# Self-attention of a hybrid decoder trunk: row maximum, exponential and transposes one PSUM bank at a time

## The chip, the cores and the metric

The kernel runs on one core of one Trainium2 chip. The metric is the device time of one execution in microseconds (us); of several runs the median is taken. TensorE is called PE here (PEld is its weight load), VectorE is DVE, ScalarE is ACT, GpSimd is POOL, SyncE is SP. PSUM has eight banks of 512 f32 values in each of 128 partitions.

## The reference, cut to what matters

Two layers of a decoder with 1024 tokens. Each layer has a causal attention of 8 heads (head width 96 for q and k, 64 for v), a state-space group, a recurrent group, an output projection, a cross-attention and an MLP. The change touches only the causal attention:

```
for one block of 128 queries and one head:
    sc = q_i @ k^T * scale                 # 128 x 1024
    sc = where(kpos <= qpos, sc, -inf)     # so only (i+1)*128 columns count
    p  = softmax(sc) = exp(sc - max) / sum(exp(sc - max))
    y  = p @ v
```

## The kernel before, in words

All data stay in SBUF with the token or the channel on the partitions, and the weights stream in. The attention of a layer is written as 64 units, `unit(n)`: four pairs of heads, in each pair eight query blocks i = 0 to 7, in each block the two heads. Unit n works on w = (i+1)*128 key columns. For i below 4 (a short unit) the scores fill one PSUM bank or less, for i of 4 to 7 (a long unit, 32 in each layer) they reach into a second. Units alternate between banks 0, 1 and banks 2, 3. The number n mod 16 is the place of a unit in its pair of heads; places 8 to 15 are the long ones.

What a unit passes through, with its lines:

- PE `scores(n)`: one f32 product of up to 512 columns for each bank (L1191), and in the last bank a small bf16 product that adds the mask (L1194). It then counts up `s_ps`.
- DVE `row_max(n)`: waits for `s_ps`, one reduction over all w columns, across both banks (L2165). It writes the negated maximum `nmx`.
- ACT `probs(n)`: waits for `nmx`, one exponential over all w columns into `prob`, with the row sum into `esum` (L1702). It counts up `s_exp`.
- PE `probs_T(n)`: waits for `s_exp`, transposes `prob` in chunks of up to four 128x128 blocks (L1207). The chunks alternate between banks 4 and 5; chunk m also waits until the copy of chunk m-2 is done (`pt_sb`).
- ACT `keep_probs_T(n)`: copies each chunk to SBUF (L1737).
- PE `outputs(g)`: after every four units, probabilities times values (L1221).

The order on each engine is written out by hand, and each engine works its own list in order. PE does scores(n+1), then sometimes outputs, then a side task, then probs_T(n). ACT does probs(n+1), a side task, then keep_probs_T(n): so the copies of unit n stand behind the exponential of unit n+1. DVE does row_max(n+1), then side tasks. The side tasks (`side_tasks`) are the q and k projections of the next heads and the state-space chunks: EL and EA (exponentials on ACT, L1718, L1722), CB and TR (DVE), Y (PE L1163, DVE L2197 and L2203), RB (the reciprocal sums: PE L1178, ACT L1726, after which DVE scales y, L2175).

POOL runs its own list beside them, mostly products and sums of two SBUF tensors: `rope_add` (L788, 32 partitions x 1024), `ssd_inputs` (L762), `decay_products` (L751, L754), `gate_z` (L795), `y_square` (L802, L805, L807), and in the last pair of heads `split_early` (L812, L815) and `split_lru` (L823, L825), which prepare operands of the output projection.

`recip_sums` (L2169) takes the reciprocal of the eight sums of half a pair of heads. `nmx`, `mx`, `rsum` and `rinv` are small SBUF tables, [128, 2, 4]; `esum` is [128, 2, 8].

Of the kernel before, what the change touches and what calls it, by code (L numbers as in the profile page):

```python
# [21 lines left out]
ALU = mybir.AluOpType  # L22
ACT = mybir.ActivationFunctionType
AX = mybir.AxisListType


P = 128
DEPTH = 2
T = 1024
HT = 512  # L30
# [35 lines left out]
def step(n):  # L66

    return n // STEPS, n % STEPS
# [62 lines left out]
def unit(n):  # L131

    return n // (2 * NBLK), (n % (2 * NBLK)) // 2, n % 2


def chunks_before(n):

    return sum(1 if unit(m)[1] < 4 else 2 for m in range(n))
# [61 lines left out]
def x_tile(n):  # L200
# [17 lines left out]
             "mix_gt": 4, "mix_rstd": 3, "mg_hi": 1, "xk_done": 8, "mv_done": 2, "mv_lo": 4, "xpt_lo": 8, "xs_exp": 8, "xpt_sb": 8, "xo_hi": 16,  # L218
             "sum_y": 4, "sum_hi": 16, "hm_sq": 64, "p1_kept": 15, "t_free0": 16, "t_free1": 16, "h_lo": 24,
             "sq_used": 24, "sum_ready": 6, "softplus_v": 3, "k_rot": 1, "conv_done": 6, "lru_xr": 2, "lru_v": 4,  # L220
             "prep": 1, "first_qk_dve": 4, "s_max": 64, "side_dve": 36, "m_ce": 8, "m_sw": 8, "m_xd": 8, "r_inv": 8,
             "m_st": 8, "y_done": 8, "mix_sum": 2, "mix_lo": 6, "mix_n": 6, "mg_v": 1, "mg_lo": 1, "xq_done": 8,
             "xs_max": 8, "xp_n": 8, "xo_lo": 16, "sum_v": 16, "hm_t": 64, "x_add": 17, "c_add": 105, "mem_sq": 2,
             "mem_sum": 1, "mem_col": 1, "mem_rstd": 1, "hm_st": 768, "a_hi": 161, "a_lo": 161, "a_sum": 60,
# [28 lines left out]
def trunk(nc, xT, memT, posb, ropec, small, final_g, wt, wv, wh, lruw, outT):  # L253
# [7 lines left out]
    def sem(name):  # L261
        return ctx.enter_context(nc.semaphore(name))

    with ctx:
# [27 lines left out]
        prob = at("prob", B + 24 * K, [P, 2, T])  # L292
# [75 lines left out]
        mx = at("mx", o + 340, [P, 2, 4])  # L368
        nmx = at("nmx", o + 372, [P, 2, 4])
        rsum = at("rsum", o + 404, [P, 2, 4])  # L370
# [4 lines left out]
        esum = at("esum", o + 760, [P, 2, NBLK])  # L375
# [4 lines left out]
        ps = ctx.enter_context(nc.psum_tensor("ps", [P, 8, HT], F32))  # L380

        def banks(b, n=2):
            return ps[:, b:b + n, :].rearrange("p b t -> p (b t)")
# [46 lines left out]
        dt_ps, prep = sem("dt_ps"), sem("prep")  # L430
# [2 lines left out]
        q_rope, q_half, k_rope, k_rope_1, k_rot = (sem(n) for n in ("q_rope", "q_half", "k_rope", "k_rope_1", "k_rot"))  # L433
        side_ps, side_a, side_v = sem("side_ps"), sem("side_act"), sem("side_dve")
        s_ps, s_max, s_exp, pt_ps, pt_sb, o_ps = (sem(n) for n in ("s_ps", "s_max", "s_exp", "pt_ps", "pt_sb", "o_ps"))
        r_inv, y_done, y_sq, y_acc = sem("r_inv"), sem("y_done"), sem("y_sq"), sem("y_acc")
        m_aU, m_cz, m_ce, m_sw, m_xd, m_st, m_z = (
            sem(n) for n in ("m_aU", "m_cz", "m_ce", "m_sw", "m_xd", "m_st", "m_z"))
# [39 lines left out]
        def cols_of(half):  # L478
            return slice(half * HT, (half + 1) * HT)

        def stat(t, n):

            i = (n // 2) % t.shape[2]
            return t[:, n % 2, i:i + 1]

        def here(counted, n, of_layer=None):

            return n + PER_LAYER[counted.name] * (layer if of_layer is None else of_layer)

        with nc.Block() as block:  # L490
# [44 lines left out]
            for layer in range(DEPTH):  # L535
# [421 lines left out]
                def _(pe):  # L957
# [116 lines left out]
                    for b in range(NBLK):  # L1074
                        last = pe.transpose(ps[:, 6, b * 32:(b + 1) * 32], ss[0:32, b * P:(b + 1) * P], ident[0:32, 0:32])
# [107 lines left out]
                    def scores(n):  # L1183

                        c, i, hh = unit(n)
                        q, k = qT[c % 2][hh], kT[c % 2][hh]
                        for j in range(0, i + 1, 4):
                            w = min(4, i + 1 - j) * P
                            dst = ps[:, 2 * (n % 2) + j // 4, 0:w]
                            edge = j + 4 > i  # L1190
                            last = pe.matmul(dst, q[0:DQ, i * P:(i + 1) * P], k[0:DQ, j * P:j * P + w],  # L1191
                                             start=True, stop=not edge)
                            if edge:
                                last = pe.matmul(ps[:, 2 * (n % 2) + j // 4, w - P:w], ident_h[:, :], future[:, :],  # L1194
                                                 start=False, stop=True)
                        last.then_inc(s_ps, 1)

                    def probs_T(n):

                        i = unit(n)[1]  # L1200
                        pe.wait_ge(s_exp, here(s_exp, n + 1))
                        for part, j0 in enumerate(range(0, i + 1, 4)):
                            m = chunks_before(n) + part
                            if m >= 2:
                                pe.wait_ge(pt_sb, here(pt_sb, m - 1))
                            for j in range(j0, min(j0 + 4, i + 1)):
                                last = pe.transpose(ps[:, 4 + m % 2, (j - j0) * P:(j - j0 + 1) * P],  # L1207
                                                    prob[:, n % 2, j * P:(j + 1) * P], ident[:, :])
                            last.then_inc(pt_ps, 1)
# [58 lines left out]
                    for j, (src, bank) in enumerate(((sq, 4), (ss, 6), (acc, 0))):  # L1268
# [8 lines left out]
                        for half in range(2):  # L1277
                            last = pe.matmul(ps[:, bank + half, :], ones[:, 0:1].to_broadcast([P, P]), src[:, cols_of(half)],
                                             start=True, stop=True)
# [21 lines left out]
                    for at_k in range(2, DC):  # L1301
# [5 lines left out]
                        for s in range(2):  # L1307
                            last = mix_products(s, at_k, 0, 1)
# [138 lines left out]
                    for s in range(2):  # L1447
# [7 lines left out]
                        w = wsp[:, s, :, :].rearrange("p a (k m) -> p a k m", m=P)  # L1455
                        for half in range(2):
                            for k in range(DC):
                                for part, a in ((0, 0), (0, 1), (1, 0)):
                                    last = pe.matmul(ps[:, 2 + half, :], w[:, part, k, :], hB[:, a, k, cols_of(half)],
                                                     start=(k == 0 and part == 0 and a == 0), stop=(k == DC - 1 and part == 1))  # L1460
# [90 lines left out]
                    for n in range(RING_FILLS):  # L1551
# [9 lines left out]
                        for q in (0, 1, 3, 2):  # L1561
                            if n == 0 and q == 2:
                                pe.wait_ge(ht_sum, here(ht_sum, 4 * NFP - 1))
                            last = operand_products(n, q)
                        last.then_inc(u_done, 1)
                    operands_ready(FILLS - 1)
                    for q in range(4):
                        if last_layer and q == 2:
                            fin_means(0)
                        for n in range(RING_FILLS, FILLS):  # L1570
                            last = operand_products(n, q)
# [6 lines left out]
                def _(act):  # L1578
# [117 lines left out]
                    def probs(n):  # L1696

                        w = (unit(n)[1] + 1) * P
                        act.wait_ge(s_max, here(s_max, n + 1))
                        if n >= 2:  # L1700
                            act.wait_ge(pt_ps, here(pt_ps, chunks_before(n - 1)))
                        act.activation(prob[:, n % 2, 0:w], banks(2 * (n % 2))[:, 0:w], ACT.Exp,  # L1702
                                       bias=stat(nmx, n), accum_out=stat(esum, n)).then_inc(s_exp, 1)

                    def side_act(kind, i):
# [276 lines left out]
                def _(dve):  # L1982
# [109 lines left out]
                    for k in range(2):  # L2092
                        last = dve.scalar_tensor_tensor(cq_s[:, k, :], cq_s[:, k, :], g("q_g", k), banks(4), ALU.mult, ALU.mult)
# [49 lines left out]
                    for ch in range(2):  # L2143
                        last = dve.scalar_tensor_tensor(gt_s[:, ch, :], gt_s[:, ch, :], g("lru_g", ch), banks(4), ALU.mult, ALU.mult)
# [15 lines left out]
                        dve.tensor_tensor(turned[NOPE:DQ, cols], ps[DQ:P, bank, :], cs[half][DQ:P, :], ALU.mult).then_inc(done, 1)  # L2160

                    def row_max(n):
                        dve.wait_ge(s_ps, here(s_ps, n + 1))
                        w = (unit(n)[1] + 1) * P
                        dve.tensor_reduce(stat(nmx, n), banks(2 * (n % 2))[:, 0:w], AX.X, ALU.max, negate=True).then_inc(s_max, 1)  # L2165

                    def recip_sums(hf):
                        dve.wait_ge(s_exp, here(s_exp, 8 * hf + 8))
                        dve.reciprocal(rinv[:, :, :], esum[:, :, 4 * (hf % 2):4 * (hf % 2) + 4]).then_inc(r_inv, 1)  # L2169

                    def keep_y(hf):
# [132 lines left out]
                    for c in range(DC):  # L2304
                        if c in (4, DC - 1):
                            n = c // 4 - (c == 4)
# [178 lines left out]
                    for n in range(2, FILLS):  # L2485
                        operand_low(n)
                        p, i = step(n - SLOTS + 1 - STEPS)
# [133 lines left out]
```

## Time and profile before

| | us |
|---|---|
| median of 3 runs | 2822.7 |
| lowest, highest | 2820.27, 2824.53 |
| the profiled execution | 2822.41 |
| its span | 2820.7 |
| PE busy in it | 2755.8 (98%) |
| DVE busy | 1477.2 (52%) |
| ACT busy | 1153.2 (41%) |
| POOL busy | 1551.8 (55%) |

The granted clock of TensorE is 0.996 of full speed over the span. "Busy" is the union of an engine's recorded instructions. Times of single rows are microseconds from the start of the span. A matmul's recorded end is modelled: in a stream without a pause the next f32 matmul of 128 columns is recorded as starting a little before the end of the one before.

### The profile page before, as it was taken

How to read it: one execution, taken by the hardware profiler on the slowest of the kernel's cores; microseconds unless marked ns; L12 is line 12 of the kernel's file. 1: busy time of each engine (PE TensorE's matmuls, PEld its weight loads, DVE VectorE, ACT ScalarE, POOL GpSimd, SP SyncE). 2: the span in 40 equal slices, each digit the busy share in tenths (PEclk: the TensorE clock that was granted, in tenths of full speed). 3: DMA queues.
4: the chain of work that ended last, by engine and by line, in shares of the span. 5: the costliest groups of instructions: out<-in, count | busy, mean ns of one | idle time of the engine just before them, and what ended most of it. 6: DMA issues, size and time to landing. Idle time of an engine off the chain costs nothing.

```text
span 2820.7 us, 33795 instructions
## 1 busy us (share of the span) xinstructions
PE 2755.8 (98%) x12974; PEld 2165.7 (77%) x12974; DVE 1477.2 (52%) x1575; ACT 1153.2 (41%) x1802; POOL 1551.8 (55%) x887
## 2 busy tenths in 40 slices
PE   8999999999999999999999999999999999999998
PEld 6766668888878887888887666688888788878886
DVE  8584456116474555445665744561265755455445
ACT  3455552224153434333324655432242434343334
POOL 4333443450357776697833344434413777767977
PEclk9999999999999999999999999999999999999999
DMA  3100011230124447676311000112201343476763
GB/s 139 50 10 6 16 38 42 78 105 8 52 95 163 145 142 242 199 243 208 110 62 42 15 1 16 39 51 90 90 16 45 127 153 139 161 248 196 237 203 119
DMA packets 175402, 292.17 MB, mean 104 GB/s; under 512 B 16656, under 2 KB 84240, under 8 KB 174608
## 3 DMA queue, kind: packets, MB, share of 16 engines
q1 hardware_dynamic: 175248, 290.08, 30.9%
q8 instruction: 101, 1.65, 0.2%
q14 instruction: 53, 0.43, 0.1%
HBM read 226.85 MB, written 63.18 MB: 103 GB/s over the span
## 4 chain that ended last, share of the span: by engine, by line
PE 85%; DVE 8%; ACT 3%; POOL 1%; issue 1%; DMA 1%; SPq 0%; DVEq 0%; ACTq 0%; POOLq 0%
PE ps L1528 21%; PE ps L1468 18%; PE ps L969 18%; PE ps L1337 6%; PE ps L1191 4%; PE ps L1221 2%; PE ps L1393 2%; PE ps L1207 2%; PE ps L1352 2%; PE ps L1368 2%; PE ps L1085 2%; DVE hT L2376 1%; DVE xbc L2056 1%; PE ps L1420 1%; PE ps L1287 1%
## 5 line engine op out<-in xcount | busy, mean ns | idle before, releaser
L1528 PE MATMUL ps<-b_op,a_op 128*128 128x512 f32 x2688 | 614.6, 391 | 11.6 <-POOL a_op L910 8.3
L1528 PEld LDWEIGHTS ps<-b_op,a_op 128*128 128x128 f32 x2688 | 506.5, 189 | 119.2 <-POOL a_op L910 9.2
L969 PE MATMUL ps<-hA,wsp 128*128 128x512 f32 x1920 | 442.3, 391 | 0.8 <-POOL wsp L724 0.7
L721 POOL TENSOR_TENSOR wsp<-raw,ones 128x1024 fp32r<-128x1024 f32 x63 | 124.4, 1975 | 555.6 <-PE ps L969 446.2
L969 PEld LDWEIGHTS ps<-hA,wsp 128*128 128x128 f32 x1920 | 360.3, 188 | 80.7 <-issue 5.3
L2420 DVE TENSOR_TENSOR b_op<-raw_b,b_op 128x1024 fp32r<-128x1024 f32 x112 | 226.6, 2024 | 294.8 <-ACT b_op L1915 294.8
L1468 PE MATMUL ps<-hT,ring 128*128 128x512 f32 x1440 | 339.2, 394 | 8.1 <-POOL ring L878 8.1
L1468 PEld LDWEIGHTS ps<-hT,ring 128*128 128x128 f32 x1440 | 270.0, 189 | 75.0 <-POOL ring L878 19.6
L1915 ACT ACTIVATE b_op<-raw_b 128x1024 fp32r<-128x1024 f32 x112 | 118.8, 1061 | 335.1 <-PE ps L1528 305.1
L1468 PE MATMUL ps<-hB,ring 128*128 128x512 f32 x1080 | 250.6, 389 | 1.1 <-POOL ring L878 1.1
L1468 PEld LDWEIGHTS ps<-hB,ring 128*128 128x128 f32 x1080 | 202.6, 188 | 44.0 <-POOL ring L878 2.0
L910 POOL TENSOR_TENSOR a_op<-kept_a,a_op 128x1024 fp32r<-128x1024 f32 x64 | 203.1, 3180 | 33.5 <-ACT a_op L1920 32.7
L878 POOL TENSOR_TENSOR ring<-raw,ring 128x512 fp32r<-128x512 f32 x112 | 156.7, 1399 | 93.0 <-ACT ring L1888 88.0
L732 POOL TENSOR_TENSOR wsp<-raw,wsp 128x1024 fp32r<-128x1024 f32 x45 | 107.7, 2394 | 136.5 <-ACT wsp L1809 133.8
L1337 PE MATMUL ps<-hA,wsp 128*128 128x512 f32 x768 | 178.1, 391 | 0.1
L724 POOL TENSOR_TENSOR wsp<-raw,wsp 128x1024 fp32r<-128x1024 f32 x63 | 167.0, 2650 | 4.9
L878 POOL TENSOR_TENSOR ring<-blk_e,ring 128x512 fp32r<-128x512 f32 x98 | 126.6, 1292 | 76.2 <-ACT ring L1888 71.8
L1337 PEld LDWEIGHTS ps<-hA,wsp 128*128 128x128 f32 x768 | 143.6, 188 | 31.5 <-issue 1.9
L2165 DVE TENSOR_REDUCE nmx<-ps 128x1 f32<-128x256 f32 (+7 forms) x128 | 96.7, 757 | 133.1 <-PE ps L1194 131.3
L910 POOL TENSOR_TENSOR a_op<-raw_a,a_op 128x1024 fp32r<-128x1024 f32 x48 | 122.7, 2557 | 75.0 <-ACT a_op L1920 75.0
L969 PE MATMUL ps<-hB,wsp 128*128 128x512 f32 x672 | 155.2, 391 | 2.1 <-DVE x L2274 2.1
L2448 DVE TENSOR_TENSOR mu<-mu,ps 128x512 f32<-128x512 f32 x90 | 62.0, 689 | 169.4 <-PE ps L1468 167.4
(335 smaller groups left out, 4426.9 us busy)
## 6 DMA issues: line engine op xcount, KB each, us to landing
raw_b<-hidden_operands SPq DMA_DIRECT2D x112, 512.0 KB, 4.9
raw<-in_weight_tiles SPq DMA_DIRECT2D x108, 512.0 KB, 3.2
raw_a<-in_weight_tiles SPq DMA_DIRECT2D x192, 256.0 KB, 3.3
hidden_operands<-hm_t SPq DMA_DIRECT2D x128, 256.0 KB, 3.6
hidden_operands<-hm_s SPq DMA_DIRECT2D x96, 256.0 KB, 2.0
raw<-in_weight_tiles SPq DMA_DIRECT2D x64, 256.0 KB, 3.2
blk_e<-in_weight_tiles SPq DMA_DIRECT2D x56, 256.0 KB, 3.3
kept_a<-in_weight_tiles SPq DMA_DIRECT2D x32, 256.0 KB, 6.0
```

The costliest lines, as they stand in the source:

```text
L721: pool.tensor_tensor(wsp[:, s, 0, :], raw[:, s, :], ones[:, 0:1].to_broadcast([P, TILE]), ALU.mult).then_inc(w_ready[s], 1)
L724: pool.tensor_tensor(wsp[:, s, 1, :], raw[:, s, :], wsp[:, s, 0, :].bitcast(F32), ALU.subtract).then_inc(w_ready[s], 1)
L732: pool.tensor_tensor(wsp[:, s, 1, :], raw[:, s, :], wsp[:, s, 0, :].bitcast(F32), ALU.subtract).then_inc(w_ready[s], 1)
L878: pool.tensor_tensor(ring[:, FILL_SLOT[i], 1, :], pair_blk(g, src), ring[:, FILL_SLOT[i], 0, :].bitcast(F32), ALU.subtract).then_inc(a_lo, 1)
L910: pool.tensor_tensor(op[:, 1, :, :], source_a(n)[:, :, :], op[:, 0, :, :].bitcast(F32), ALU.subtract)\
L969: last = pe.matmul(ps[:, 2 * buf + half, 0:n], w[:, k, col:col + P], rhs(part, k, half * n, n), start=(at_k == 0 and w is w_hi and part == 0),
L1191: last = pe.matmul(dst, q[0:DQ, i * P:(i + 1) * P], k[0:DQ, j * P:j * P + w], start=True, stop=not edge)
L1337: last = pe.matmul(ps[:, 2 * (g % 2) + half, :], w[:, part, k, :], hA[:, a, k, half * HT:(half + 1) * HT], start=(k == 0 and part == 0 and ...
L1468: last = pe.matmul(ps[:, M_BANK[p], :], w[:, part, k, :], rhs(a, k), start=(k == 0 and part == 0 and a == 0), stop=(k == 3 and part == 1))
L1528: last = pe.matmul(ps[:, 4 * (1 - p % 2) + q, :], w[:, part, q // 2, r, (q % 2) * P:(q % 2 + 1) * P], h[:, a, r, :], start=(s == 0 and r = ...
L1915: act.activation(b_op[op_slot(n)][:, 0, :, :], raw_b[n % SLOTS][:, :, :], ACT.Copy).then_inc(b_hi, 1)
L2420: dve.tensor_tensor(op[:, 1, :, :], raw_b[n % SLOTS][:, :, :], op[:, 0, :, :].bitcast(F32), ALU.subtract)\
```

## The change

For long units the work goes bank by bank. PE counts up a new semaphore `s_ps_a` after the product of the first bank. DVE reduces the first bank as soon as that is there, into the table `mx`; then the second bank into `nmx`; then it waits for its own two results and joins them with a minimum (both are negated) of two 128x1 SBUF operands. ACT takes the exponential of the first bank and then of the second, as two instructions with a sum each: the first sum goes to `rsum`, the second to `esum`. PE may begin the transposes of the first four blocks after the first exponential (`s_exp_a`) and those of the rest after the second. Before the reciprocal of a half whose units are long, DVE adds the two tables of sums. Short units do what they did.

```
 def scores(n):
+    else:                                   # not the last bank
+        last.then_inc(s_ps_a, 1)
 def probs_T(n):
-    pe.wait_ge(s_exp, here(s_exp, n + 1))
     for part, j0 in enumerate(range(0, i + 1, 4)):
+        if part == 0 and i >= 4:
+            pe.wait_ge(s_exp_a, here(s_exp_a, long_before(n) + 1))
+        else:
+            pe.wait_ge(s_exp, here(s_exp, n + 1))
 def probs(n):
-    act.activation(prob[:, n % 2, 0:w], banks(2 * (n % 2))[:, 0:w], ACT.Exp,
+    if unit(n)[1] < 4:
+        act.activation(prob[:, n % 2, 0:w], ps[:, 2 * (n % 2), 0:w], ACT.Exp,
+                       bias=stat(nmx, n), accum_out=stat(esum, n)).then_inc(s_exp, 1)
+        return
+    act.activation(prob[:, n % 2, 0:HT], ps[:, 2 * (n % 2), :], ACT.Exp,
+                   bias=stat(nmx, n), accum_out=stat(rsum, n)).then_inc(s_exp_a, 1)
+    act.activation(prob[:, n % 2, HT:w], ps[:, 2 * (n % 2) + 1, 0:w - HT], ACT.Exp,
                    bias=stat(nmx, n), accum_out=stat(esum, n)).then_inc(s_exp, 1)
 def row_max(n):
+    w = (unit(n)[1] + 1) * P
+    if unit(n)[1] < 4:
+        dve.wait_ge(s_ps, here(s_ps, n + 1))
+        dve.tensor_reduce(stat(nmx, n), ps[:, 2 * (n % 2), 0:w], AX.X, ALU.max, negate=True).then_inc(s_max, 1)
+        return
+    dve.wait_ge(s_ps_a, here(s_ps_a, long_before(n) + 1))
+    dve.tensor_reduce(stat(mx, n), ps[:, 2 * (n % 2), :], AX.X, ALU.max, negate=True).then_inc(s_mx, 1)
     dve.wait_ge(s_ps, here(s_ps, n + 1))
-    w = (unit(n)[1] + 1) * P
-    dve.tensor_reduce(stat(nmx, n), banks(2 * (n % 2))[:, 0:w], AX.X, ALU.max, negate=True).then_inc(s_max, 1)
+    dve.tensor_reduce(stat(nmx, n), ps[:, 2 * (n % 2) + 1, 0:w - HT], AX.X, ALU.max, negate=True).then_inc(s_mx, 1)
+    dve.wait_ge(s_mx, here(s_mx, 2 * long_before(n) + 2))
+    dve.tensor_tensor(stat(nmx, n), stat(nmx, n), stat(mx, n), ALU.min).then_inc(s_max, 1)
 def recip_sums(hf):
     dve.wait_ge(s_exp, here(s_exp, 8 * hf + 8))
+    if hf % 2:
+        dve.tensor_tensor(esum[:, :, 4:8], esum[:, :, 4:8], rsum[:, :, :], ALU.add).then_inc(s_sum2, 1)
+        dve.wait_ge(s_sum2, here(s_sum2, hf // 2 + 1))
```

## Rows read from the trace of the kernel before

**Rows 1.** Stretches of the pairs of heads, layer 0: length, busy (count) by engine.

```profile
197.00:249.00 52.00, 50.69 (x312) 31.56 (x312) 23.71 (x46) 32.69 (x76) 23.24 (x24) 1.00 0.03 7
249.00:301.00 52.00, 51.00 (x328) 31.80 (x326) 22.22 (x44) 30.31 (x70) 21.80 (x21) 1.00 0.00 1
...
353.00:402.00 49.00, 43.70 (x322) 28.92 (x320) 23.62 (x40) 25.14 (x58) 28.93 (x22) 1.00 0.00 1
```

**Rows 2.** Timeline, unit 30: start, length, engine, line [idle before <-releaser].

```profile
290.79 1.22 DVE L2165 TENSOR_REDUCE nmx<-ps 128x1 f32<-128x1024 f32 x1 [4.50 <-PE ps L1194]
292.05 1.11 ACT L1702 ACTIVATE prob<-ps,nmx 128x1024 f32<-128x1024 f32 x1 [2.24 <-DVE nmx L2165]
293.16 0.97 ACT L1737 ACTIVATE probT<-ps 128x512 f32<-128x512 f32 x2
293.89 0.30 PE L1207 MATMUL ps<-ident,prob 128*128 128x128 f32 x1 [0.26 <-ACT probT L1737]
```

**Rows 3.** Groups by shape, DVE, whole span: count | busy, mean ns | idle before.

```profile
L2165 DVE TENSOR_REDUCE nmx<-ps 128x1 f32<-128x1024 f32 x16 | 19.6, 1225 | 35.8 <-PE ps L1194 35.8
L2165 DVE TENSOR_REDUCE nmx<-ps 128x1 f32<-128x512 f32 x16 | 11.1, 692 | 25.1 <-PE ps L1194 25.1
L2165 DVE TENSOR_REDUCE nmx<-ps 128x1 f32<-128x256 f32 x16 | 6.7, 421 | 9.5 <-PE ps L1194 9.2
L2165 DVE TENSOR_REDUCE nmx<-ps 128x1 f32<-128x128 f32 x16 | 4.5, 291 | 3.7 <-PE ps L1194 2.5 <-DVE xbc L2203 1.2
```

**Rows 4.** Groups by shape, ACT line L1702, whole span.

```profile
L1702 ACT ACTIVATE prob<-ps,nmx 128x1024 f32<-128x1024 f32 x16 | 17.8, 1115 | 23.9 <-DVE nmx L2165 23.9
...
L1702 ACT ACTIVATE prob<-ps,nmx 128x512 f32<-128x512 f32 x16 | 11.0, 688 | 9.0 <-DVE nmx L2165 8.8
```

**Rows 5.** Timeline, 59 to 64 us, small DVE instructions beside POOL.

```profile
59.22 1.89 POOL L721 TENSOR_TENSOR wsp<-raw,ones 128x1024 fp32r<-128x1024 f32 x1 [6.03 <-PE ps L969]
59.31 1.82 DVE L2001 TENSOR_TENSOR lr<-lr,c 128x2 f32<-128x2 f32 x1
61.16 0.16 DVE L2002 SCALAR_TENSOR_TENSOR c<-spt,lr 128x2 f32<-128x2 f32 x1
61.19 2.39 POOL L724 TENSOR_TENSOR wsp<-raw,wsp 128x1024 fp32r<-128x1024 f32 x1
61.36 2.25 DVE L2072 TENSOR_SCALAR c<-c 128x2 f32<-128x2 f32 x1
```

**Rows 6.** Timeline, units 26 and 27.

```profile
278.03 0.59 ACT L1726 ACTIVATE rbs<-ps 128x512 f32<-128x512 f32 x1
279.33 0.95 DVE L2165 TENSOR_REDUCE nmx<-ps 128x1 f32<-128x768 f32 x1
280.31 0.90 ACT L1702 ACTIVATE prob<-ps,nmx 128x768 f32<-128x768 f32 x1 [1.04 <-DVE nmx L2165]
281.68 0.87 ACT L1737 ACTIVATE probT<-ps 128x512 f32<-128x512 f32 x2
282.42 0.84 PE L1207 MATMUL ps<-ident,prob 128*128 128x128 f32 x6
```

**Rows 7.** Timeline, unit 12.

```profile
229.43 2.37 POOL L788 TENSOR_TENSOR qT<-qT,q_tmp 32x1024 f32<-32x1024 f32 x1
229.62 1.09 DVE L2165 TENSOR_REDUCE nmx<-ps 128x1 f32<-128x896 f32 x1 [1.69 <-PE ps L1194]
230.74 1.01 ACT L1702 ACTIVATE prob<-ps,nmx 128x896 f32<-128x896 f32 x1 [0.54 <-DVE nmx L2165]
```

**Rows 8.** Timeline, unit 56.

```profile
368.62 0.82 DVE L2165 TENSOR_REDUCE nmx<-ps 128x1 f32<-128x640 f32 x1
369.32 1.89 POOL L812 TENSOR_TENSOR w_early<-raw_early,ones 128x1024 fp32r<-128x1024 f32 x1
369.48 0.79 ACT L1702 ACTIVATE prob<-ps,nmx 128x640 f32<-128x640 f32 x1 [1.41 <-DVE nmx L2165]
371.39 1.74 PE L1221 MATMUL ps<-probT,v_tok 128*64 128x256 f32 x16 [0.48 <-ACT probT L1737]
```

More of the change, by code:

```diff
@@ L133, in unit, with long_before @@
     return n // (2 * NBLK), (n % (2 * NBLK)) // 2, n % 2
+def long_before(n):
+    return sum(1 for m in range(n) if unit(m)[1] >= 4)
 def chunks_before(n):
@@ L220 @@
              "sq_used": 24, "sum_ready": 6, "softplus_v": 3, "k_rot": 1, "conv_done": 6, "lru_xr": 2, "lru_v": 4,
-             "prep": 1, "first_qk_dve": 4, "s_max": 64, "side_dve": 36, "m_ce": 8, "m_sw": 8, "m_xd": 8, "r_inv": 8,
+             "prep": 1, "first_qk_dve": 4, "s_max": 64, "s_ps_a": 32, "s_mx": 64, "s_exp_a": 32, "s_sum2": 4, "side_dve": 36, "m_ce": 8, "m_sw": 8, "m_xd": 8, "r_inv": 8,
              "m_st": 8, "y_done": 8, "mix_sum": 2, "mix_lo": 6, "mix_n": 6, "mg_v": 1, "mg_lo": 1, "xq_done": 8,
@@ L435, in trunk @@
         s_ps, s_max, s_exp, pt_ps, pt_sb, o_ps = (sem(n) for n in ("s_ps", "s_max", "s_exp", "pt_ps", "pt_sb", "o_ps"))
+        s_ps_a, s_mx, s_exp_a, s_sum2 = (sem(n) for n in ("s_ps_a", "s_mx", "s_exp_a", "s_sum2"))
         r_inv, y_done, y_sq, y_acc = sem("r_inv"), sem("y_done"), sem("y_sq"), sem("y_acc")
```

## The prediction

> **What bounds the kernel now.** I read the page first: PE is busy 98% of the span, and most of the chain that ended last is PE, so a change is worth what it does to PE's pauses. The change touches only the attention, so I cut that into its four pairs of heads. [rows 1] gives, after the length of each stretch, the busy time of PE, PEld, DVE, ACT and POOL. PE lacks 1.31, 1.00 and 5.30 us in the first, second and last pair, and the third repeats the second (1.00): 8.6 us in layer 0. Layer 1 has the same pattern at the same places, so about 17 us of pauses lie in reach, 0.6% of the time. Everywhere else in the attention PE works without a pause, and what DVE and ACT do there is hidden as long as they are not later than PE.
>
> Then I went along PE's pauses in the timeline. In each of the first three pairs three of them stand at the end, places 14 and 15 (0.2 to 0.5 us each). The rest are in the last pair. [rows 2] shows the kind, unit 30, place 14: the reduction runs 290.79 to 292.01, the exponential follows at 292.05 for 1.11 us, then ACT goes straight into the two copies of the transposes of unit 29 (293.16), and PE begins the transposes of unit 30 at 293.89. The first copy takes half of the 0.97 us and ends at about 293.65; PE comes 0.2 us after that. So PE waits here for the copy that frees the bank, and this copy stands on ACT behind the whole exponential. The reader is to see that an early release of the first half of the exponential does not reach PE in such a place.
>
> **The change part by part.**
>
> *Reductions.* One reduction of 1024 columns costs 1.225 us, one of 512 0.692, of 256 0.421, of 128 0.291 [rows 3]; for 384 I take 0.56, midway between 256 and 512. If the first bank is reduced while PE still works on the second, only the second reduction lies after the scores, plus the join. The join is a DVE instruction of 128x1 on two SBUF operands. The nearest row is 0.16 us for 128x2 (the instruction at 61.16) [rows 5]; with 0.03 for its wait 0.20 us. So the exponential starts 1.225 - 0.692 - 0.20 = 0.33 us earlier for i = 7, and by the same slope for i = 6. For i = 4 the second product is over long before the first reduction is, and nothing is won; for i = 5 about 0.18.
>
> *Exponentials.* 1024 columns cost 1.115 us, two of 512 cost 2 x 0.688 = 1.376 [rows 4]: 0.26 us more, which is the part of an instruction that does not grow with its columns, so I take the same for every long unit. ACT starts its next instruction at the end of these lengths, so I take them whole. It comes to 64 x 0.26 = 17 us on ACT, which is 60% busy here [rows 1]; only the places count where PE stands behind ACT.
>
> *Net on the chain of [rows 2].* The start is 0.33 earlier, the end 0.26 later on top: the copy, and PE behind it, come 0.07 us earlier. This is nearly nothing, 0.07 in each of the first three pairs.
>
> *Place 11 (units 11, 27, 43).* [rows 6], unit 27: the reduction begins at 279.33 not because of the scores but because DVE has just scaled y, which waited for ACT's instruction at 278.03, which stood behind the exponential of unit 26. That one ends 0.22 later after the change (0.26 longer, 0.04 earlier), so the reduction begins at 279.55. Both halves then lie in series: 0.692 + 0.03 + 0.421 + 0.03 + 0.16 = 1.33 against 0.95; the exponential starts at 280.93 instead of 280.31, ends 0.26 later on top, and with the side exponential behind it the copies come at 282.56 instead of 281.68, 0.88 later. PE's transposes at 282.42 follow the first copy without any slack (PE has no pause there now, but the copy ends only 0.11 us before the first weight load), so PE is delayed 0.84. In sum + 0.8 in each of the first three pairs.
>
> *The join beside POOL.* [rows 5] shows DVE instructions of 128x2 with SBUF operands. 0.16 us is what they take undisturbed. The one at 59.31 takes 1.82 and ends at 61.13, POOL's two-operand instruction having run 59.22 to 61.11; the one at 61.36 takes 2.25 under POOL's next, which ends at 63.58. One that asks between the two gets through (61.16). So an instruction with two SBUF operands that asks after POOL has begun waits until about 0.14 before POOL's recorded end, whatever its size. The reductions from PSUM run beside POOL at their usual length [rows 7, 8]. The join is of the first kind, and it is new on the path; the units before the change had nothing of the sort there.
>
> I laid the 64 joins of the timeline against POOL. Most fall free. *Unit 12* [rows 7]: second reduction over at 229.62 + 0.56 = 230.18, the join asks at 230.21. POOL's L788 runs 229.43 to 231.80 (0.22 later after the change, since it hangs on the scaled y). The join ends at about 232.04, the exponential starts at 232.08 instead of 230.74, and ends 0.26 later on top: + 1.6. Side exponential, copies and PE follow, since ACT has no pause there. This takes the 0.84 of unit 11 into itself: 1.5 for the first pair. In the second and third pair L788 comes after the join of place 12, so they stay at 0.8.
>
> *Unit 56* [rows 8]: DVE comes free at about 368.5, reduces 0.69 and 0.29, the join asks at 369.54, POOL's L812 has begun at 369.32 and ends at 371.21. The join ends at 371.24; the exponential starts at 371.28 instead of 369.48 and ends at + 2.06. On ACT the side exponential and the copy of unit 55 follow directly, and PE's outputs at 371.39 already wait for that copy: + 2.05 us. Here L812 hangs on the same DVE instruction that frees DVE for the reductions, so the two keep their distance.
>
> *The rest of the last pair*: unit 59 repeats place 11 (+ 0.84), but PE's pause of 0.5 us before the outputs behind it takes most of it. For units 61, 62 and 63 it depends on tenths of a microsecond whether the join falls beside one of POOL's long instructions; free it is + 0.1, held + 1.9 at the end. I take 0.95. Last pair: 3.0.
>
> *The other edits.* The added PE waits stand in PE's queue ahead of instructions that already have one; beside the present double wait of probs_T PE runs on without a pause, so nothing; if not, 64 times a few hundredths. The eight added sums of tables stand before the reciprocals, may be held up to 0.7 us by L795, and are followed by RB 5 us later: nothing. What waits behind a held join on DVE are side tasks with more than 1 us to spare.
>
> **The sum.** One layer: 1.5 + 0.8 + 0.8 + 3.0 = 6.1; both 12.2. After the attention PE's chain goes on without a reserve that could take it back. On the profiled execution: 2822.4 + 12.2 = 2834.6; that execution lies 0.3 below the median, so 2835.
>
> The Trainium skill (GPSIMD Engine Reference, Specifications) says that POOL's SBUF interfaces are shared with VectorE, with contention for DVE instructions that have two SBUF inputs. It gives no price. Read as sharing cycles, it would have the join merely lengthened by its own 0.16 us, and the sum would be that of the first rival; the trace says it is held to the end of POOL's instruction.
>
> **The rivals.** (a) *The join is not held*, being only one column, or the joins fall between POOL's instructions. For: one at 61.16 got through. Against: 128x2 is nearly as small and was held. Only place 11 is left, 0.8 x 3 - 0.07, and about 0.1 in the last pair: 2.5 a layer, 2828. (b) *All joins of the last pair are held*: 1.5 + 0.8 + 0.8 + 2.05 + 1.9 = 7.1 a layer, 14 us, and a further one elsewhere 1 or 2 more: 2837 to 2840. (c) *Faster*: the first exponential releases the transposes of places 14 and 15, because the exponential and not the copy is PE's gate. Then PE comes 0.33 + 1.115 - 0.688 = 0.76 earlier in each of three pairs, about 1.5 in the last, 3.8 a layer: 2815, if place 11 costs nothing. For: the profile names the exponential as what the weight loads waited for. Against: [rows 2], PE starts half a microsecond after the exponential's end and 0.2 after the first copy's. It decides if the transposes of unit 30 start before the first copy.
>
> **How the numbers follow.** Forecast 0.55, (a) 0.2, (b) 0.14, (c) 0.11. The bounds of the last pair (2.1 to 4.0) and of unit 12 (0.8 to 1.5) alone give 9 to 14 us; (a) reaches down to 5, place 11 with some slack to 3. Range 2826 to 2841. What the measurement tells from no change is 0.2%, 5.6 us, here 2828.3; (a) is split by it. Faster 0.1, the same 0.15, slower 0.75.
>
> **What would show it.** Right: joins of 0.16 us mostly, of 1 to 2 us at units 12 and 56; the exponential of unit 27 at + 0.6; PE's pause before the outputs of unit 56 grown by 2 us; PE's first transposes of place 14 unmoved against its scores. Wrong: all joins short (then (a)); the transposes of unit 30 before the first copy (then (c)); a reduction of 512 columns slowed while PE writes the next bank.

## The result and the profile after

| | before | after |
|---|---|---|
| median, us | 2822.70 (5 runs) | 2840.40 (6 runs) |
| lowest, highest | 2820.27, 2824.63 | 2837.03, 2841.93 |
| the profiled execution | 2822.41 | 2838.73 |
| its span | 2820.7 | 2837.0 |
| PE busy | 2755.8 | 2760.1 |
| DVE busy | 1477.2 | 1517.8 |
| ACT busy | 1153.2 | 1167.9 |

The change makes the kernel slower: ratio 1.0062, with a 95% interval of 1.0051 to 1.0072. One run of the kernel before (3464.89 us) and one of experiment 8 (3463.72 us) fell into a slow state of the chip and are left out of the medians. I forecast + 12.2 us; the profiled execution shows + 16.3 and the medians + 17.7. The direction and most of the mechanism held; a term of about 5 us was missing.

Where the time went is read first by pairs, as in [rows 1]. The cuts are moved by the delay that had built up. The columns are again the length, and the busy time of PE, PEld, DVE, ACT and POOL; the number ahead of the DMA share is the granted clock.

```profile
197.00:251.00 54.00, 51.48 (x318) 31.89 (x317) 28.00 (x63) 34.18 (x92) 23.04 (x24) 1.00 0.03 7
251.00:305.00 54.00, 52.51 (x329) 32.61 (x330) 25.80 (x61) 32.14 (x86) 21.84 (x21) 1.00 0.00 1
305.00:358.00 53.00, 51.50 (x336) 32.58 (x336) 26.05 (x62) 32.91 (x88) 23.14 (x22) 1.00 0.06 21
358.00:412.00 54.00, 45.28 (x304) 29.44 (x302) 32.30 (x57) 26.32 (x72) 28.92 (x22) 0.91 0.00 1
```

PE now lacks 2.52, 1.49, 1.50 and 8.72 us, against 1.31, 1.00, 1.00 and 5.30: + 1.21, + 0.49, + 0.50 and + 3.42. The reader is to see the last line's clock too, 0.91 where [rows 1] has 1.00. The whole attention of each layer, cut at the same instructions in both kernels, splits the loss into pauses and slower work. First the changed kernel, layer 0 and layer 1, same columns:

```profile
196.77:411.75 214.98, 200.74 (x1276) 126.39 (x1276) 112.38 (x242) 125.78 (x338) 97.18 (x89) 0.98 0.02 7
1599.55:1821.25 221.70, 207.47 (x1305) 129.84 (x1304) 116.21 (x246) 131.50 (x345) 101.63 (x91) 0.98 0.04 12
```

and the kernel before:

```profile
197.00:402.00 205.00, 196.39 (x1276) 124.14 (x1276) 91.78 (x174) 118.44 (x274) 97.08 (x89) 1.00 0.03 8
...
1590.00:1805.00 215.00, 206.41 (x1305) 129.17 (x1304) 95.58 (x178) 124.13 (x281) 101.67 (x91) 0.99 0.04 12
```

The number of products is the same (1276 and 1305). What PE lacks went from 8.61 to 14.24 in layer 0 and from 8.59 to 14.23 in layer 1: pauses + 11.3 us together. The same products took 4.35 and 1.06 us longer: + 5.4. That is 16.7; 0.4 of it comes back outside the attention.

**The groups** (form xcount | busy, mean ns of one | idle before) answer to [rows 3, 4]:

```profile
L2186 DVE TENSOR_REDUCE mx<-ps 128x1 f32<-128x512 f32 x64 | 44.1, 689 | 47.5 <-PE ps L1197 45.6
L2190 DVE TENSOR_TENSOR nmx<-nmx,mx 128x1 f32<-128x1 f32 x64 | 34.3, 536 | 2.2
L1717 ACT ACTIVATE prob<-ps,nmx 128x512 f32<-128x512 f32 x64 | 44.1, 689 | 81.4 <-DVE nmx L2190 81.1
L1719 ACT ACTIVATE prob<-ps,nmx 128x512 f32<-128x512 f32 x16 | 10.9, 679 | 0.0
```

The reduction of 512 columns costs 0.689 with PE writing the bank beside it, against 0.692 in [rows 3], so PE's writes do not slow it. The join costs 0.536 on average, where a free one has 0.16: the mean hides two kinds. Of the 64 joins 24 begin while a POOL instruction runs that has more than 0.2 us left; all 24 last until that instruction's recorded end and 0.01 to 0.02 us more. The other 40 take 0.16 to 0.18. Which of the held ones cost time has to be looked for one by one in the timeline (start, length; in brackets the idle time and its releaser). Unit 12, the answer to [rows 7]:

```profile
229.38 0.56 DVE L2188 TENSOR_REDUCE nmx<-ps 128x1 f32<-128x384 f32 x1
229.40 2.35 POOL L794 TENSOR_TENSOR qT<-qT,q_tmp 32x1024 f32<-32x1024 f32 x1
229.97 1.80 DVE L2190 TENSOR_TENSOR nmx<-nmx,mx 128x1 f32<-128x1 f32 x1
231.81 0.69 ACT L1717 ACTIVATE prob<-ps,nmx 128x512 f32<-128x512 f32 x1 [1.12 <-DVE nmx L2190]
```

A join of one column, begun at 229.97, ends at 231.77, with POOL's instruction (231.75). Unit 56, against [rows 8], is the same thing and the dearest:

```profile
371.41 1.89 POOL L818 TENSOR_TENSOR w_early<-raw_early,ones 128x1024 fp32r<-128x1024 f32 x1
371.64 1.68 DVE L2190 TENSOR_TENSOR nmx<-nmx,mx 128x1 f32<-128x1 f32 x1
373.35 0.69 ACT L1717 ACTIVATE prob<-ps,nmx 128x512 f32<-128x512 f32 x1 [3.19 <-DVE nmx L2190]
...
375.51 2.79 PE L1232 MATMUL ps<-probT,v_tok 128*64 128x256 f32 x12 [2.49 <-ACT probT L1754]
```

Unit 30, against [rows 2]: a free join, two exponentials in a row, then the copies, then PE.

```profile
293.27 0.16 DVE L2190 TENSOR_TENSOR nmx<-nmx,mx 128x1 f32<-128x1 f32 x1
293.47 0.69 ACT L1717 ACTIVATE prob<-ps,nmx 128x512 f32<-128x512 f32 x1 [1.91 <-DVE nmx L2190]
294.15 0.68 ACT L1719 ACTIVATE prob<-ps,nmx 128x512 f32<-128x512 f32 x1
294.81 0.98 ACT L1754 ACTIVATE probT<-ps 128x512 f32<-128x512 f32 x2
295.55 0.63 PE L1218 MATMUL ps<-ident,prob 128*128 128x128 f32 x4 [0.16 <-ACT probT L1754]
```

PE's transposes come 0.74 after the copy has begun and 1.39 after the first exponential's end. The early release is not used: in both layers the transposes of places 14 and 15 start 0.74 us after the first of these copies, as in the kernel before.

The delay of PE's first transposes against the kernel before, taken unit by unit from start times, gives the ladder. Layer 0: + 0.49 at unit 11, + 1.31 at 12, + 1.21 from 14; + 1.93 at 27, + 1.66 from 30; + 2.39 at 43, + 2.12 from 46; + 5.74 at 56, + 6.20 at 60, + 7.42 at 63; PE is + 9.75 when the attention is over (it transposes the reciprocals at 411.44, before at 401.69). In layer 1 the first pair costs 1.44 and the second and third 0.45 each again, unit 56 costs 2.02 and not 3.62, and the end is at + 16.22 (1814.34 against 1798.12).

**The missing part** shows where the clock is cut finely. Same columns, the changed kernel:

```profile
370.00:375.60 5.60, 3.05 (x17) 1.76 (x17) 5.39 (x8) 2.27 (x7) 4.80 (x3) 1.00 0.02 3
375.60:379.00 3.40, 3.40 (x17) 1.98 (x18) 0.25 (x2) 1.13 (x4) 0.13 (x1) 0.50 0.00 0
402.90:409.70 6.80, 4.99 (x24) 3.29 (x26) 1.56 (x4) 2.66 (x6) 0.00 (x0) 0.50 0.00 0
1805.80:1812.60 6.80, 4.97 (x22) 3.28 (x24) 1.58 (x4) 2.68 (x6) 0.00 (x0) 0.50 0.00 0
```

0.50 of full speed is the lower level, 1.2 GHz. Until 375.51 PE had stood for 2.49 us; until 401.60 it had stood for 1.93, ahead of the second fall, and inside that stretch it stands 1.36 more. The kernel before has one such stretch in the two attentions, 3.4 us from 1793.4, behind pauses of 0.58, 1.48 and 0.74 us; behind nearly the same three in layer 0 (0.59, 1.48 and 0.74) it has none. PE's work inside runs at half speed: 3.40 + 4.99 + 4.97 - 3.40 = 10.0 us of it more than before, half of that is 5.0 us, and 5.4 is what the same products took longer. The other runs of the changed kernel have a mean clock of 0.992 to 0.995, the profiled one 0.995, so some of them probably hold more such stretches; they have no trace.

### The profile page after: what moved, and what is told of

It is laid out like the page before. It is cut to its first block, busy times and chain, and to the rows that moved or that the text cites. A ratio compares the mean times of both kernels' runs of the same rounds, so it can differ in the third digit from the quotient of the medians.

```text
span 2837.0 us, 34123 instructions
## 1 busy us (share of the span) xinstructions
PE 2760.1 (97%) x12974; PEld 2167.0 (76%) x12974; DVE 1517.8 (54%) x1711; ACT 1167.9 (41%) x1930; POOL 1551.7 (55%) x887
## 4 chain that ended last, share of the span: by engine, by line
PE 83%; DVE 9%; ACT 4%; POOL 1%; issue 1%; DMA 1%; SPq 0%; DVEq 0%; ACTq 0%; POOLq 0%
PE ps L1539 21%; PE ps L1479 18%; PE ps L975 17%; PE ps L1348 6%; PE ps L1197 3%; PE ps L1232 2%; PE ps L1404 2%; PE ps L1363 2%; PE ps L1379 2%; PE ps L1091 2%; PE ps L1218 1%; DVE hT L2404 1%; DVE xbc L2073 1%; PE ps L1431 1%; PE ps L1298 1%
## 5 line engine op out<-in xcount | busy, mean ns | idle before, releaser
L975 PEld LDWEIGHTS ps<-hB,wsp 128*128 128x128 f32 x672 | 126.0, 188 | 29.9 <-issue 3.8
```

Of the source, the lines that this page charges most:

```text
L975: last = pe.matmul(ps[:, 2 * buf + half, 0:n], w[:, k, col:col + P], rhs(part, k, half * n, n), start=(at_k == 0 and w is w_hi and part == 0),
```

## The experiments

The comparisons have their own runs of the kernel before, with medians of 2822.36 to 2822.44.

**1. The join by another instruction.** Both halves' maxima lie side by side, and one reduction over two columns with a single SBUF input joins them.

```
-         mx = at("mx", o + 340, [P, 2, 4])
-         nmx = at("nmx", o + 372, [P, 2, 4])
+         both = at("both", o + 340, [P, 2, 2, 4])
+         mx, nmx = both[:, 0, :, :], both[:, 1, :, :]
...
- dve.tensor_tensor(stat(nmx, n), stat(nmx, n), stat(mx, n), ALU.min)
+ dve.tensor_reduce(stat(nmx, n), both[:, :, n % 2, (n // 2) % 4], AX.X, ALU.min)
```

> The changed kernel with its join written as a reduction over two columns of one SBUF table (one SBUF input) instead of a minimum of two SBUF operands. Nothing else differs. Theory (the join is held by POOL because it has two SBUF inputs): a reciprocal with one SBUF input ran beside POOL at its usual 0.2 us, so all 128 joins take about 0.2 us; unit 12 and unit 56 lose nothing, PE's long pauses of the last pair go, and with them the half-speed stretches of TensorE. What is left is place 11 and the longer exponentials: 0.45 in each of the first three pairs, about 0.3 in the last, so 2 to 4 us above the kernel before, some 2826. Rival (the two exponentials on ACT are the cost): as slow as the changed kernel, 2840, joins short or not. Rival (any small SBUF instruction on DVE is held): joins still 1 to 2 us at units 12 and 56, 2840.

Measured: 2825.14, ratio 1.0011 (1.0002 to 1.0020). The long units are 32 a layer, so there are 64 joins and not the 128 that the expectation says. Their group in this kernel:

```profile
L2190 DVE TENSOR_REDUCE both<-both 128x1 f32<-128x2 f32 x64 | 9.9, 155 | 2.2
```

Not one is held: at unit 12 it begins at 229.41 under a POOL instruction that runs from 228.83 for 2.36 us, and takes 0.16. Here too 24 of the 64 begin while a POOL instruction has more than 0.2 us left, and each of them takes 0.15 to 0.16. So about 15 of the 17.7 us go with the form of one tiny instruction. What is left is + 0.4 a pair, from place 11, and 0.49 at unit 56. The expectation missed in one point: half-speed stretches do not all go. In the profiled execution 3.4 us of layer 0's attention and 6.8 of layer 1's run at half speed, against 3.4 in all before.

It is shown that this form of the join is not held, and that neither its size nor its wait nor the moment was the cause. The edit changes two things at once, the operation and the number of SBUF inputs, and the trace of the kernel before separates them:

```profile
199.97 1.04 POOL L762 TENSOR_TENSOR aU_lo<-tri_le,att_l 128x512 fp32r<-128x512 f32 x1
200.46 0.69 DVE L2156 TENSOR_TENSOR q_tmp<-ps,cs 64x512 f32<-64x512 f32 x1 [1.34 <-PE ps L1085]
...
371.29 2.36 POOL L815 TENSOR_TENSOR w_early<-raw_early,w_early 128x1024 fp32r<-128x1024 f32 x1
371.69 0.19 DVE L2169 RECIPROCAL rinv<-esum 128x8 f32<-128x8 f32 x1
```

A TENSOR_TENSOR with one input in PSUM runs at its usual 0.69 beside POOL, so it is not the operation as such. Of the TENSOR_TENSORs with both inputs in SBUF that begin there while a POOL instruction has more than 0.2 us left, 119 of them, none ends before POOL's. But one SBUF input is not enough to be free. The reciprocal above is, and the reduction. The TENSOR_SCALAR at 61.36 in [rows 5] has one SBUF input as well and was held for 2.25 us, and so was a copy from SBUF to SBUF (L2213, which still runs 0.55 us after POOL's end).

**2. Exponentials split, one reduction.** No join.

```
- dve.wait_ge(s_ps_a, ...); dve.tensor_reduce(stat(mx, n), ...)
- dve.wait_ge(s_ps, ...);   dve.tensor_reduce(stat(nmx, n), ...)
- dve.wait_ge(s_mx, ...);   dve.tensor_tensor(...)
+ dve.wait_ge(s_ps, here(s_ps, n + 1))
+ dve.tensor_reduce(stat(nmx, n), banks(2 * (n % 2))[:, 0:w], AX.X, ALU.max, negate=True)
```

> The exponentials and transposes bank by bank as in the changed kernel, with the two sums, but the row maximum as one reduction as before: no join. Theory: only the 0.26 us more on ACT per long unit counts. At places 14 and 15 PE stands behind ACT, + 0.26 there; at place 11 two exponentials and the scaled y in a chain, + 0.5. So + 0.5 to 0.8 a pair of heads, 4 to 6 us in all, 2828. Rival (exponentials are the whole cost): 2840. Rival (c) of the prediction (the early release helps PE): below 2822.

Measured: 2827.47, ratio 1.0018 (1.0008 to 1.0028), + 5.1 us. Unit 30 here:

```profile
293.36 0.68 ACT L1717 ACTIVATE prob<-ps,nmx 128x512 f32<-128x512 f32 x1
294.02 0.98 ACT L1752 ACTIVATE probT<-ps 128x512 f32<-128x512 f32 x2
294.76 1.06 PE L1216 MATMUL ps<-ident,prob 128*128 128x128 f32 x8 [0.51 <-ACT probT L1752]
```

PE starts 0.74 after the first copy has begun, as in every kernel here that leaves ACT's order alone. The split exponential brings nothing and costs 0.26 where ACT is what PE waits for: + 0.55 a pair.

**3. Reductions split, one exponential, the join with two inputs.**

```
- act.activation(prob[:, n % 2, 0:HT], ...).then_inc(s_exp_a, 1)
- act.activation(prob[:, n % 2, HT:w], ...)
+ act.activation(prob[:, n % 2, 0:w], banks(2 * (n % 2))[:, 0:w], ACT.Exp, ...)
...                                       # PE waits for s_exp alone
```

> The row maximum bank by bank with the two-operand join as in the changed kernel, but one exponential and one wait of PE as before. Theory: the holds stay. Unit 12 about + 1.0 us, unit 56 + 1.8, units 61 to 63 one or two holds more, and TensorE falls to half speed after the longer pauses; places 14 and 15 gain 0.3 a pair. Each layer + 4 to 6 us, 8 to 12 in all, 2833. Rival (exponentials are the cost): at or below the kernel before, 2820 to 2823.

Measured: 2836.04, ratio 1.0043 (1.0029 to 1.0057). The joins have a mean of 535 ns again; up to unit 12 1.0 us is lost, and at unit 56 3.2 to 3.4, its join taking 1.68 and a half-speed stretch following in both layers. In its profiled execution four stretches at half speed lie in the two attentions, 20.5 us in sum.

**4. The same with the join of experiment 1.**

```
- dve.tensor_tensor(stat(nmx, n), stat(nmx, n), stat(mx, n), ALU.min)
+ dve.tensor_reduce(stat(nmx, n), both[:, :, n % 2, (n // 2) % 4], AX.X, ALU.min)
```

> The row maximum bank by bank with the join as a reduction of one SBUF input, one exponential as before. Theory: neither holds nor longer exponentials. Places 14 and 15 start 0.3 us earlier, place 11 (DVE busy before it) is up to 0.4 later, the last pair gains about 0.3: in sum within 3 us of the kernel before, likelier below it, 2821. Rival (any small SBUF instruction is held): as the third kernel, 2833. Rival (the reading of one bank by DVE while PE writes the next slows one of them): the scores or the first reductions take longer than before and the time is above 2828.

Measured: 2819.86, ratio 0.9994 (0.9985 to 1.0003). Per pair + 0.20 at place 11, then - 0.15 and - 0.34 at places 12 and 14; no stretch at half speed in either attention. Against experiment 3 this is one instruction for another, and 16 us. The early reduction was the good part of the change: in PE's start times it gains about 0.3 in a pair. In the time of the whole kernel that is not clear of the noise, as the interval holds 1.

**5. Only unit 56's join with two inputs.** Experiment 1 with

```
+ if n == 56:
+     dve.tensor_tensor(...)      # the join of the change
+ else:
+     dve.tensor_reduce(...)      # the join of experiment 1
```

> The first experiment (all joins as reductions, both exponentials) with the two-operand join put back in unit 56 alone, once in each layer. Theory: that join asks 0.2 us after POOL's L812 has begun and is held 1.5 us; PE's outputs of unit 56 come 2.0 us later than in the first experiment in both layers. In layer 0 of the changed kernel TensorE fell to half speed for 3.41 us right behind this pause and 3.6 us were lost instead of 2.0: if the pause is what brings that, it shows again here, in sum 4 us above the first experiment plus up to 1.7 us for each half-speed stretch of 3.41 us that is added: 2829 to 2833. Rival (the clock falls through something else, later joins or chance): 2.0 us in each layer and no stretch at 375 us, 2829.

Measured: 2833.33, ratio 1.0036 (1.0022 to 1.0049): 8.2 us above experiment 1 for two held joins, one in each layer, which are 1.5 us each longer than a free one (1.68 against 0.16). The five runs fall into two sorts: 2829.43 and 2830.04 at a mean clock of 0.995 and 0.996, and 2833.33, 2833.99 and 2834.04 at 0.993 and 0.994. The profiled one is the lowest. In it

```profile
370.71 1.68 DVE L2191 TENSOR_TENSOR both<-both 128x1 f32<-128x1 f32 x1
...
374.59 1.63 PE L1232 MATMUL ps<-probT,v_tok 128*64 128x256 f32 x14 [2.50 <-ACT probT L1754]
```

PE stands 2.50 us before the outputs that follow unit 56's scores, and no half-speed stretch follows in layer 0 (+ 1.99 from unit 48 to 56); in layer 1 the same pause is followed by one (+ 3.52). The pause does not decide it alone. Only the lowest has a trace, so where the clock fell in the others is not seen. The two tables lie side by side here as in experiment 1, so their place in SBUF was not what cured the join. The price of a held join is its delay in some executions, and more where TensorE's clock falls behind it.

**6. POOL starts after the join.** The change as it is, and POOL's first instruction of that place waits for the join of unit 56.

```
+ pool.wait_ge(s_max, here(s_max, 57))
  split_early(0, w_early)
```

> The changed kernel with one wait added on POOL: the first instruction of the early weight split (L812 of the kernel before) waits until the join of unit 56 is done, once in each layer. DVE, ACT and PE are as in the changed kernel, two-operand joins included. Theory: the join of unit 56 takes 0.16 us instead of 1.68, PE's outputs of unit 56 come 2 us earlier in each layer, and where the half-speed stretch behind it goes, 1.7 us more; the join of unit 57 may now be held by the next instruction of POOL, which has 1.7 us of slack before PE. In sum 3 to 7 us below the changed kernel, 2833 to 2837. Rival (the joins are slow by themselves, not through POOL): unchanged, 2840.

Measured: 2834.58, ratio 1.0040 (1.0026 to 1.0053), 5.8 us below the changed kernel.

```profile
371.68 0.16 DVE L2191 TENSOR_TENSOR nmx<-nmx,mx 128x1 f32<-128x1 f32 x1
371.92 1.89 POOL L818 TENSOR_TENSOR w_early<-raw_early,ones 128x1024 fp32r<-128x1024 f32 x1 [0.43 <-DVE nmx L2191]
...
374.03 1.73 PE L1233 MATMUL ps<-probT,v_tok 128*64 128x256 f32 x16 [0.97 <-ACT probT L1755]
```

The join takes 0.16 and unit 56 costs 0.47 and 0.49 in the two layers. The later holds stay: the joins of units 60 to 63 take 0.70, 2.24, 1.59 and 1.19 beside POOL's later instructions, as in the changed kernel (0.71, 2.25, 1.60, 1.19), and 10.2 us in each layer run at half speed around the attention's end, where the changed kernel has 6.8. A two-input join is cured by order only one place at a time.

**7. Early reduction only where it gains.** Experiment 4 for query blocks 6 and 7; the others as in the kernel before, one reduction and one wait.

```
- return sum(1 for m in range(n) if unit(m)[1] >= 4)
+ return sum(1 for m in range(n) if unit(m)[1] >= 6)
...
- if unit(n)[1] < 4:
+ if unit(n)[1] < 6:
```

> The fourth experiment (row maximum bank by bank, join as a reduction, one exponential) but only for query blocks 6 and 7, where the scores of the second bank take longest; blocks 4 and 5 have one reduction as before. Theory: place 11 no longer pays its 0.2 us and places 14 and 15 keep their 0.34 in each pair: about 0.2 x 3 x 2, 1 us better than the fourth experiment, 2818 to 2820. Rival (place 11's loss was made good at place 12 anyway): equal to the fourth.

Measured: 2819.53, ratio 0.9989 (0.9980 to 0.9998). The profiled execution, 2814.89, is the lowest of eleven, with no stretch at half speed in either attention.

```profile
290.18 0.15 DVE L2182 TENSOR_REDUCE both<-both 128x1 f32<-128x2 f32 x1
290.37 1.11 ACT L1711 ACTIVATE prob<-ps,both 128x1024 f32<-128x1024 f32 x1 [1.90 <-DVE both L2182]
292.21 1.06 PE L1216 MATMUL ps<-ident,prob 128*128 128x128 f32 x8
```

Place 11 costs nothing now and places 12 and 14 keep their gain, - 0.5 a pair. It beats both kernels; against the one before the interval only just leaves 1.

**8. A copy between the halves.** Would the early release help if ACT used it? Experiment 7, and for places 14 and 15 the exponential in halves, with the first copy of the unit before between them:

```
  order on ACT, before: exp(n+1), copy 0 of n, copy 1 of n
+ exp first half(n+1), copy 0 of n, exp second half(n+1), copy 1 of n
```

> The kernel of the experiment on late units, and in the units of places 14 and 15 the exponential in two halves, with the copy of the unit before's first chunk moved between the halves on ACT, so that the early release can reach PE (the transposes wait for that copy). The two sums are joined for these units. Theory: the first transposes of places 14 and 15 come about 0.5 us earlier than before instead of 0.34, and in the last pair up to 0.8: 2 to 3 us below the experiment on late units, 2815 to 2818. Rival (the pauses move to the second chunk, whose half of the exponential now stands behind the copy): no gain over it, 2819.

Measured: 2820.47, ratio 0.9990 (0.9981 to 1.0000), not told apart from experiment 7.

```profile
291.43 0.59 ACT L1766 ACTIVATE probT<-ps 128x512 f32<-128x512 f32 x1
291.91 0.69 ACT L1721 ACTIVATE prob<-ps,both 128x512 f32<-128x512 f32 x1
292.51 1.33 PE L1228 MATMUL ps<-ident,prob 128*128 128x128 f32 x8
...
297.50 2.81 PE L1242 MATMUL ps<-probT,v_tok 128*64 128x256 f32 x24 [0.41 <-ACT probT L1766]
```

PE starts these transposes while the second exponential runs, so the waits of the change do work once the copy is early. But of the 0.69 gained in a pair by place 15 only 0.28 is left, since the second copy is later and PE then waits 0.41 for it. ACT's order, not its granularity, is the lever, and it only moves the pause.

**9. The changed kernel once more,** for a second trace of its clock.

> The changed kernel once more, for a second trace of its granted clock. If the half-speed stretches follow directly and always from PE's pauses, they stand at the same places: 3.41 us behind unit 56 in layer 0 only, 6.83 us at the end of each attention. If a pause only makes them possible, some will be at other places or missing, and the time of a run moves with them by about 1.7 us for 3.41 us of half speed.

Measured: 2836.42, span 2834.7, 2.3 us shorter than the first profile. Same columns as in the windows above:

```profile
370.00:375.60 5.60, 3.04 (x19) 1.92 (x19) 5.33 (x8) 2.24 (x7) 4.93 (x3) 1.00 0.02 3
375.60:379.00 3.40, 3.40 (x26) 2.25 (x21) 0.00 (x0) 2.24 (x7) 0.70 (x1) 1.00 0.00 0
400.90:407.80 6.90, 5.06 (x24) 3.36 (x26) 1.59 (x4) 2.69 (x6) 0.00 (x0) 0.51 0.00 0
```

The first window is the same to 0.01 us of PE's work, and the pause before these outputs is 2.50 us here. In the second the same code goes on at full clock, 26 products where the other execution did 17. Behind the last pair the fall is there in both.

**Pauses and clock apart.** Each profiled execution against that of the kernel before, over both attentions, from the first transposes of unit 0 to those of the last reciprocals, with the same cut as above into what PE lacks and what the same products take. The medians include executions that have no trace, and the clock outside the attentions, so they need not follow the sum.

| | PE's pauses, us | the same products, us |
|---|---|---|
| the change | + 11.3 | + 5.4 |
| the change once more (9) | + 11.2 | + 3.7 |
| 1, join as a reduction | + 2.9 | + 3.1 |
| 2, exponentials split | + 4.6 | + 1.3 |
| 3, reductions split | + 6.6 | + 6.7 |
| 4, the same, join as a reduction | - 1.7 | - 2.8 |
| 5, one two-input join a layer | + 5.9 | + 3.0 |
| 6, POOL waits | + 7.3 | + 7.1 |
| 7, blocks 6 and 7 only | - 3.0 | - 3.2 |
| 8, copy between | - 2.8 | + 1.5 |

The pauses are the steady part: the two executions of the changed kernel agree to 0.1 us in them and differ by 1.7 in the other column. Of the + 11.3 the join's form is 8.4.

## Why the prediction came out as it did

**PE is the bound and the pauses are what counts: right.** All of the loss but 0.4 us lies in the two attentions, in PE's pauses and its clock.

**Places 14 and 15, no gain from the release: right** (experiment 2). Rival (c) is out: the transposes of these places never come before the first copy, and experiment 8 shows what it would have taken.

**Place 11: right in place, and in its size for itself.** + 0.72 at unit 27, forecast + 0.84 (its exponential begins 0.47 later than before, without the delay already built up, forecast 0.62). But places 12 and 14 give 0.27 of it back, where I had reckoned 0.07, so the second and third pair cost 0.45 and not 0.8: 1.4 us too much over four pairs. Experiment 4 shows whose gain that is: the early reduction's.

**Unit 12: right**, 1.44 for the first pair against 1.5. **Unit 56: right as a delay**, 2.02 in layer 1 against 2.05.

**The last units: the held case came.** From 57 to 63 the transposes lost 1.68 in layer 0 against 0.95, which was the middle between a free join (0.1) and a held one (1.9). Six of the eight joins of the last pair are held, as rival (b) had it. Only one of those after unit 56 adds a pause clearly, that of unit 62 (+ 1.35):

```profile
397.58 1.90 POOL L818 TENSOR_TENSOR wsp<-raw_early,ones 128x1024 fp32r<-128x1024 f32 x1
397.88 1.60 DVE L2190 TENSOR_TENSOR nmx<-nmx,mx 128x1 f32<-128x1 f32 x1
399.52 0.69 ACT L1717 ACTIVATE prob<-ps,nmx 128x512 f32<-128x512 f32 x1 [2.68 <-DVE nmx L2190]
```

The join of unit 61 is the longest of all, 2.25, and PE is not later behind it. I had also overlooked that one-input POOL instructions hold the join: that of unit 60 took 0.71 under a cast, that of unit 28 0.72 under a copy. Neither cost PE a pause.

```profile
283.42 1.04 POOL L792 COPY qT<-q_tmp 32x1024 f32<-32x1024 f32 x1
...
283.75 0.72 DVE L2190 TENSOR_TENSOR nmx<-nmx,mx 128x1 f32<-128x1 f32 x1
```

**The step that failed** is in the sum: "Last pair: 3.0", carried into "One layer: 1.5 + 0.8 + 0.8 + 3.0 = 6.1", with each pause of PE priced at its length. In pauses this was near: 12.2 forecast, 11.3 measured, though partly by luck, since the forecast was 0.9 a layer too high for the first three pairs (3.1 against 2.2 measured) and 0.4 too low for the last (3.0 against 3.42). It has no term for what PE does behind a pause. In place of nothing the rows show the 1.2 GHz stretches: 5.4 us of slower work in the profiled execution and 3.7 in the other. [rows 1] could not have shown it, as its clock is 1.00 throughout; but the kernel before already has such a stretch behind the last and longest pauses of layer 1, at 1793.4, and that was the row to look for. Rival (b) gave 2837 to 2840 and was nearest in its number. Its joins are held as it says, but it has no term for the clock either, and the pauses alone stayed below even my own sum.

**The join beside POOL: right**, and the point of the whole case. One row that it was taken from was misread: the TENSOR_SCALAR at 61.36 in [rows 5] has one SBUF input, so that row is no case of two. The Trainium skill (GPSIMD Engine Reference, Specifications) tells of contention between the two engines for VectorE instructions with two SBUF inputs, or in a 2-port perf mode. On the first condition the trace agrees: all 24 joins with two SBUF inputs that began under POOL were held, and none of the 24 written with one. On the second no run here is a test. The hold is not a share of cycles but the rest of POOL's instruction: 1.80 and 1.68 us for an operation of 0.16.

**Open:** what decides that the clock falls behind unit 56 in one execution and not in the next. Two executions of the same kernel show both, with PE's work in the window before alike (3.05 and 3.04 us). The two layers of the kernel before, with nearly the same three pauses, show both as well. Open too is what makes some one-input DVE instructions wait for POOL and not others; here the reduction and the reciprocal did not, a TENSOR_SCALAR and a copy did.

## What to carry to other kernels

A small DVE instruction put on the critical path is priced by the engine beside it: if it has two SBUF inputs and POOL works with long instructions, expect up to POOL's instruction length each time, or write it in a form that the trace shows free, here a reduction over two columns. One input alone is no promise: look for the form in the trace, beside a POOL instruction. Before splitting an instruction for an earlier release, find what really lets the consumer start; here it was a copy further down the same queue. And where an edit makes PE's longest pauses longer, put a term for the clock behind it into the sum, with both its values.

## What was not expected of the hardware

- TensorE's fall to 1.2 GHz behind a pause of 2.5 us came in one execution of the same kernel (375.6, 3.4 us) and not in another; behind the denser pauses at the attention's end it came in both.
- One-input POOL instructions hold a two-input DVE instruction as well (0.72 under a copy of 1.04, 0.71 under a cast). A DVE reduction over two SBUF columns is not held at all, in 24 of 24 cases under POOL.
- A one-input DVE instruction can be held too: 2.25 us for a TENSOR_SCALAR of 128x2, while a reciprocal of 128x8 took 0.19 under POOL.
